# The even mixer of a two-block network as one stream on TensorE, its output product in two passes

## The reference

```python
def mixer_even(x, w_in, gla_wg2, gla_bg, gla_norm_g, w_o):
    gq, gk, gv, gg, gr, dq, dk, dv = _split(x @ w_in, EVEN_SPLITS)   # 512 512 1024 16 1024 1536 1536 1536
    o_a = gla(gq, gk, gv, gg, gla_wg2, gla_bg)          # 4 heads, keys 128, values 256
    o_a = rms_norm(o_a, gla_norm_g) * jax.nn.silu(gr)
    for g, (window, dilation) in enumerate(DIL_PAIRS):  # 3 groups x 4 heads x 128
        o_g, lse_g = dilated_branch(dq[:, :, g], dk[:, :, g], dv[:, :, g], window, dilation)
    wts = jax.nn.softmax(jnp.stack(lses, 0), axis=0)
    o_b = jnp.sum(wts[..., None] * jnp.stack(outs, 0), axis=0)
    return jnp.concatenate([o_a, o_b], axis=-1) @ w_o

def gla(q, k, v, g1, w_g2, b_g):                        # chunks of 64 tokens
    log_a = jax.nn.log_sigmoid(g1 @ w_g2 + b_g) / GLA_TAU
    b = jnp.cumsum(log_a, axis=2)
    q_dec, k_inv, k_end = q * dk ** -0.5 * exp(b), k * exp(-b), k * exp(b_last - b)
    o_intra = tril(q_dec @ k_inv.T) @ v
    s_loc = k_end.T @ v                                 # states, then a scan with the decay
    return o_intra + q_dec @ s_prev
```

## Time and profile before

| | us |
|---|---|
| three runs | 3624.05, 3625.61, 3627.94 (median 3625.61) |
| the profiled execution | 3624.08 |
| its span, first to last instruction | 3622.2 |
| TensorE busy in the span | 3477.5 (96%) |
| VectorE, ScalarE busy | 1951.2 (54%), 1618.7 (45%) |
| stretch between the input and the output projection of the even mixer | 352.72 to 459.89 |

### The profile page before, as it was taken

One profiled execution on the slowest core, in us unless ns is written; L12 is line 12 of the kernel. 1 busy time (PEld: TensorE's weight loads), 2 busy tenths in 40 slices (PEclk: granted clock), 3 DMA queues, 4 the chain that ended last, 5 costly groups with the idle time before them and its releaser, 6 DMA issues.

```text
span 3622.2 us, 43342 instructions
## 1 busy us (share of the span) xinstructions
PE 3477.5 (96%) x15818; PEld 2837.3 (78%) x15818; DVE 1951.2 (54%) x2307; ACT 1618.7 (45%) x2052; POOL 288.8 (8%) x402
## 2 busy tenths in 40 slices
PE   8999689999999989999999999999989899999997
PEld 7887578888888778777888878877878778888886
DVE  4444365555555565666575544557544745555555
ACT  4444234444444346553444444436545544444443
POOL 0000000000000000001291003000270000000000
PEclk9999799999999999999999999999999999999998
DMA  7665056665655555446655656655544456566663
GB/s 244 188 189 163 1 174 205 198 190 180 198 187 182 175 156 176 123 153 174 197 183 182 197 162 204 201 173 177 182 152 125 147 176 190 190 189 191 190 190 105
DMA packets 335046, 630.04 MB, mean 174 GB/s; under 512 B 33212, under 2 KB 35488, under 8 KB 333392
## 3 DMA queue, kind: packets, MB, share of 16 engines
q1 hardware_dynamic: 330416, 611.59, 54.4%
q0 software_dynamic: 4512, 16.86, 1.5%
HBM read 624.99 MB, written 2.33 MB: 173 GB/s over the span
## 4 chain that ended last, share of the span: by engine, by line
PE 90%; DVE 4%; POOL 3%; ACT 1%; issue 1%; DMA 0%; SPq 0%; DVEq 0%; ACTq 0%
PE psum L259 27%; PE psum L261 27%; PE psum L260 27%; PE psum L329 2%; POOL big L1274 1%; PE psum L510 1%; PE psum L512 1%; PE psum L511 1%; DVE weights_lo L221 1%; POOL scratch L1276 1%; POOL scratch L1275 1%; PE psum L918 0%; DVE x L1889 0%; PE psum L2754 0%; DVE x L1938 0%
## 5 line engine op out<-in xcount | busy, mean ns | idle before, releaser
L221 DVE TENSOR_TENSOR weights_lo<-weights_raw,weights_hi 128x1024 fp32r<-128x1024 f32 x1155 | 1419.4, 1244 | 1174.9 <-ACT weights_hi L214 1173.7
L214 ACT CAST weights_hi<-weights_raw 128x1024 fp32r<-128x1024 f32 x1155 | 1208.3, 1050 | 1653.3 <-PE psum L261 1633.0
L259 PE MATMUL psum<-weights_hi,act_hi 128*128 128x512 f32 x3112 | 1234.2, 397 | 12.8 <-DVE weights_lo L221 8.4
L261 PE MATMUL psum<-weights_hi,act_lo 128*128 128x512 f32 x3112 | 1216.4, 391 | 0.0
L260 PE MATMUL psum<-weights_lo,act_hi 128*128 128x512 f32 x3112 | 1215.2, 390 | 0.0
L259 PEld LDWEIGHTS psum<-weights_hi,act_hi 128*128 128x128 f32 x3112 | 586.7, 189 | 135.5 <-issue 15.2
L261 PEld LDWEIGHTS psum<-weights_hi,act_lo 128*128 128x128 f32 x3112 | 586.1, 188 | 124.7
L260 PEld LDWEIGHTS psum<-weights_lo,act_hi 128*128 128x128 f32 x3112 | 586.9, 189 | 116.9
L259 PE MATMUL psum<-weights_hi,hid_hi 128*128 128x512 f32 x1336 | 532.6, 399 | 16.6 <-DVE weights_lo L221 15.3
L260 PE MATMUL psum<-weights_lo,hid_hi 128*128 128x512 f32 x1336 | 523.2, 392 | 0.0
L261 PE MATMUL psum<-weights_hi,hid_lo 128*128 128x512 f32 x1336 | 523.1, 392 | 0.0
(11 more groups left out here) (396 smaller groups left out, 1796.2 us busy)
## 6 DMA issues: line engine op xcount, KB each, us to landing
weights_raw<-in_ffn_wgu SPq DMA_DIRECT2D x352, 512.0 KB, 4.4
weights_raw<-in_w_ff SPq DMA_DIRECT2D x256, 512.0 KB, 4.2
weights_raw<-in_ffn_wd SPq DMA_DIRECT2D x176, 512.0 KB, 3.8
weights_raw<-in_even_w_in SPq DMA_DIRECT2D x120, 512.0 KB, 3.7
weights_raw<-in_odd_w_in SPq DMA_DIRECT2D x64, 512.0 KB, 3.7
weights_raw<-in_w_in SPq DMA_DIRECT2D x64, 512.0 KB, 3.8
weights_raw<-in_odd_w_o SPq DMA_DIRECT2D x32, 512.0 KB, 3.8
weights_raw<-in_w_out SPq DMA_DIRECT2D x32, 512.0 KB, 3.8
```

Source lines behind the costliest of these rows:

```text
L214: nc.scalar.copy(w_hi[:, u % SPLIT_SLOTS, :size], raw[:, u % RAW_SLOTS, :size]).then_inc(hi_ready, 1)
L221: nc.vector.tensor_tensor(w_lo[:, u % SPLIT_SLOTS, :size], raw[:, u % RAW_SLOTS, :size], w_hi[:, u % SPLIT_SLOTS, :size].bitcast(F32), ALU ...
L259: nc.tensor.matmul(o, ah, wh, start=(k + j == 0), stop=False)
L261: last = nc.tensor.matmul(o, al, wh, start=False, stop=(k + j == kts - 1))
```

## The change

Everything of the even mixer now stands as side work in one stream of 137 units (`mixer_stage`, `EVEN_ENDS`). The tile `proj_e` is gone: each block goes to where it is used, q, k and the dilated q, k by way of one block-wide tile `raw_e` and turns two and three units later. Columns are loaded in the order q, k, gate, v, v, r, r, dilated q, k, v. The gate's steps have units 18 to 30, the states 36 to 42, the eight items 44 to 53, the dilated turns 58 to 99, the wide items' scores 101 to 115 and turns 103 to 118. The output product becomes a first pass over the eight gated tiles (units 121 to 136, from `hid_hi`), with the wide items' products beside it at units 123 to 130, and a second pass over the four dilated tiles (units 137 to 144). Each pass adds into x. The minimum of the negated scores replaces the maximum and its negation. The constants are loaded after the lead's turns; the vectors of the first layer norm when the first wide item is done.

```diff
@@ SyncE
+        for col, cols in ((G_K, BLK), (G_G, 16), (G_V, BLK), (G_V + BLK, BLK)):
             block_load(sp, c, w, 0, KT_D, col, cols)
...
-        project(A["even_w_o"][0], 0, [(BLK * j, BLK) for j in range(1, 4)], 12)
+        for j in range(11):
+            block_load(sp, c, w, 0, KT_D, G_R + j * BLK, BLK)
+        for row, kts in ((0, 8), (1024, 4)):
+            for j in range(4):
+                block_load(sp, c, A["even_w_o"][0], row, kts, j * BLK, BLK)
@@ GpSimd
+        pool.wait_ge(turned, LEAD)
...
-        pool.wait_ge(att_done, 8)
+        pool.wait_ge(att_done, 1)
         vectors(0, "ln1", 0)
@@ the stage
+    EVEN_ENDS = [8, 16, 17, 25, 33, 41, 49, 57, 65, 73, 81, 89, 97, 105, 113, 121, 125, 129, 133, 137]
+    EVEN_BLOCKS = [(KT_D, BLK), (KT_D, 16)] + [(KT_D, BLK)] * 13 + [(8, BLK)] * 4
@@ ScalarE, even_act: e is the unit that TensorE has just done
+            if e in (7, 15, 56, 64, 72, 80, 88, 96):
+                evac_at(act, c, e, b, lambda m, o: nc.scalar.copy(raw_e[:, m, :], o))
...
+            if e in (104, 112, 120):
+                g = (e - 104) // 8
+                evac_at(act, c, e, b, lambda m, o: nc.scalar.copy(dv[:, m, g, :], o))
+            i = (e - 102) // 2
+            if 0 <= i < 8 and e % 2 == 0:
+                least, total, _ = (d_stat[:, k, i:i + 1] for k in range(3))
+                act.wait_ge(att_scaled, i + 1)
+                of = d_sc[:, i % 2, 0:384 * (i % 2 + 1)]
+                A_(of, of, ACT.Exp, bias=least, scale=-1.0, accum_out=total).then_inc(att_exped, 1)
+            if wide_turn(e) is not None:
+                i, (t0, _) = wide_turn(e)
+                act_turn(act, c, wide_pt(i, t0, 3))
@@ VectorE
+        mixer_stage(c, even_dve, EVEN_ENDS)
+        mixer_splits(unit_lo, dve, c, EVEN_BLOCKS)
+        residual(4, 1, None)
+        c.stage(None)
...
@@ VectorE, even_dve
+            if e in (124, 128, 132, 136):
+                q = slice((e - 124) // 4 * BLK, (e - 120) // 4 * BLK)
+                evac_at(dve, c, e, b, lambda m, o: STT(out=x[:, m, q], in0=x[:, m, q], scalar=ALPHA, in1=o,
+                                                       op0=ALU.mult, op1=ALU.add))
@@ TensorE, even_pe: v is the unit just done
+            if v in (9, 10, 17, 18, 58, 59, 66, 67, 74, 75, 82, 83, 90, 91, 98, 99):
+                at_v = max(a for a in (9, 17, 58, 66, 74, 82, 90, 98) if a <= v)
+                if v == at_v:
+                    taken(pe, c, v - 2)
+                tiles(raw_e, 2 * (v - at_v))
...
+            if wide_turn(v) is not None:
+                i, (t0, t1) = wide_turn(v)
+                if t0 == 0:
+                    pe.wait_ge(att_exped, i + 1)
+                c.item_turn[i] = c.n["turn"]
+                turn(pe, c, [d_sc[:, i % 2, t * P:(t + 1) * P] for t in range(t0, t1)])
+            i = (v - 101) // 2
+            if 0 <= i < 8 and v % 2:
+                h, m = i // 2, i % 2
+                if i == 0:
+                    all_turned()
+                else:
+                    pe.wait_ge(att_scaled, i)
+                nk = P * (m + 1)
+                flat = psum[:, 6:8, :].rearrange("p b n -> p (b n)")
+                for g in range(3):
+                    last = MM(flat[:, g * nk:(g + 1) * nk], dqT[:, 4 * g + h, m * P:(m + 1) * P], dkT[:, 4 * g + h, :nk],
+                              start=True, stop=True)
+                last.then_inc(att_scored, 1)
+            i = v - 123
+            if 0 <= i < 8:
...
+                for t in range(3 * (m + 1)):
+                    last = MM(psum[:, 6 + i % 2, 0:P], wide_pt(i, t), dv[:, t % (m + 1), t // (m + 1), h * P:(h + 1) * P],
+                              start=(t == 0), stop=(t == 3 * m + 2))
+                last.then_inc(att_pved, 1)
...
+        for _ in range(4):
+            block_mm(pe, c, 8, BLK, hT_hi, hT_lo)
+        all_turned()
+        c.stage(None)
+        for _ in range(4):
+            block_mm(pe, c, 4, BLK, aT_hi, aT_lo)
```

761 lines of the change are left out of this document (292 added, 469 removed).

## The result

The changed kernel takes **3573.28 us** (median of four runs, 3571.5 to 3576.83), the kernel before 3625.05: a ratio of 0.9857, 95% interval 0.984 to 0.9874. The forecast was 3582, the range 3566 to 3600. The profiled execution took 3576.83 us with a span of 3574.6; this was the longest of its four runs; the first experiment shows where most of that lies.

A forecast was written before the change was run, and what follows sets the result against it. A chain of short steps over three engines bounds the gap, TensorE the stream. Costs 56.6 + 1.5 + 8.1 + 2.5 = 68.7, less 109.7 and 2.5, give -43.5 us: 3582 us, range 3566 to 3600.

The forecast's parts named there:

- turns of four tiles, 24: Even mixer's stream: 24 four-tile turns moved between units cost 0.48 us each, 11.5 us.
- four local states: Even mixer's stream: four states of three half-height products cost 1.26 us each, 5.0 us.
- gated items: Even mixer's stream: eight masked score and output items cost 11.5 us, plus 3.0 for entering at ten places, 14.5.
- wide items with the waits on exponentials: Even mixer's stream: 72 blocks at 0.30 us and 36 turned tiles cost 25.6 us; exponentials add 1.5 of waiting.
- second pass, waits: Output product: TensorE waits 5.3 us after the first short block and 1.4 at two others, 8.1 in all.
- second pass, clock and the rest: Output product: slow products at a reduced clock behind the 5.3 us wait cost 2.5 us, between 0 and 2.8.
- start: Kernel start: loading masks and constants after the lead's turns brings x sooner, saving 2.5 us, between 0 and 3.5.
- What bounds it: Old even mixer: a chain of short steps over three engines bounds the gap, TensorE the stream; 109.7 us open to change.
- forecast's upper bound of 62 us: Attention work in the stream: 0.4 us more at all 30 entries with products beyond the bare passes, against 56.6 expected.
- Free steps: Even mixer: norm gain, gate product and first-pass adds hide on ScalarE or VectorE inside units; uncovered adds would be 5.1 us.
- stream did not leak: Rival, wide items: ScalarE one unit later at each of eight returns 22 us, 3604 us (3592 to 3612); chance 0.15.
- Cheaper than counted: Rival, whole change: no entry cost, clock stays, long wait only 1.4, best start; 3567 us (3560 to 3568); chance 0.12.

The follow-up runs named there:

- the first experiment: The changed kernel run once more, unaltered, as yardstick for the variants beside it; 3573.16 us, ratio 0.9859 to the kernel before.
- evac_first: The changed kernel with VectorE evacuating the first pass's last output block one unit earlier, ahead of the second pass's first add; 3568.22 us, ratio 0.9846.
- late_add: evac_first, plus each second-pass add of the even mixer placed behind both splits of its two-unit block; 3565.97 us, ratio 0.9836.
- warm_tail: The changed kernel plus twenty identity products on TensorE between the second pass's first two blocks, inside the 5.02 us wait; 3571.13 us, one execution.

## Why the prediction was right, point by point

The change of the profiled executions was -47.3 us (3624.08 to 3576.83), and of the medians -51.8; forecast -43.5. Of the 8.3 us between -43.5 and -51.8, 5.3 lie up to the last output product (-48.8), the rest of the program took 1.2 back, and the other 4 are the distance of the two profiled executions from their medians, which is luck. The mechanism and the places were right; the sizes:

| term | predicted us | measured us |
|---|---|---|
| turns of four tiles, 24 | 11.5 | 11.5 (24 x 0.48) |
| four local states | 5.0 | 5.1 |
| gated items | 14.5 | 11.6 |
| wide items with the waits on exponentials | 25.6 + 1.5 | 22.8 |
| second pass, waits | 8.1 | 7.2 |
| second pass, clock and the rest | 2.5 | 2.9 |
| start | -2.5 | -0.7 |

A turn is measured as in the earlier trace rows: a unit with one in front recurs after 3.20 us (215.06 to 218.27, 250.60 to 253.81). The measured rows above the start sum to 61.1 us; from the lead turn at 30.98 to 478.90 are 447.9 us, less 321.1 + 65.3 at the bare pace 61.5. So 0.4 us are not assigned. The parts, point by point:

- **What bounds it.** Right. The gap was handing round, not work: put among the units the same work costs about 51 us where the gap and its surplus took 109.7. From the first input product to the last output product it is 465.6 us (13.23 to 478.86), forecast 472.
- **Gated items.** From the first score at 153.33 to the unit at 185.52 lie eight units (21.8 us) and seven of the eight products' items, so 10.4; with the last, 11.6. The row of 1.43 us per item held; of the 3.0 us added for entries 0.2 are left.
- **Wide items.** From the unit at 322.35 to the one at 429.95 are 107.6 us with 31 units (84.3); less one turn of the output 22.8, waits included. What was mis-sized is the price of a block, 0.30 us from the odd mixer's items: they hold two products over 64 rows, which cost 0.28 and 0.29 us more for the changes of height. Without these (3.04 - 0.57 - 0.33)/9 is 0.24, and in the even mixer, whose wide items have none, it is 0.24 too (22.8 less 1.5 of waits and 4.0 for 36 tiles, over 72), of which 0.22 is the block. The earlier trace rows had shown 0.24; it was taken as the lower bound and was the nearer row, since it is of operations that moved. These two terms, gated and wide items, are the 7 us by which the stream beat the forecast. The forecast's upper bound of 62 us can't be redone: 0.4 us at 30 entries on top of 48.5 is 60.5.
- **Waits on exponentials.** 1.5 in sum, as predicted, but 0.78 for the one with the table load in front (predicted 0.4) and 0.37 twice (predicted 0.5).

The row of ScalarE behind the first of them, in the changed kernel:

```profile
332.95 1.28 ACT L1392 ACT_TABLE_LOAD   x1
334.24 0.61 ACT L1392 ACTIVATE big<-big,big 128x384 f32<-128x384 f32 x1
```

The exponential starts 1.29 us after the load began. The Trainium skill (ScalarE: Activation LUTs, "What ACT_TABLE_LOAD costs") has 2.66 us with a drain; by that the wait would have been 2.2 us. The trace disagrees again.
- **Second pass.** One wait of 5.02 (predicted 5.3) and two of 1.10 (predicted 1.4), in the order predicted, shown by evac_first and late_add. The clock behind the long one 1.9 (predicted 2.5), shown by warm_tail. The remaining 1.0 of the tail is in slower first products and in the pace's rounding; I didn't take it apart.
- **Free steps.** Right: TensorE has no wait in the stream but those for the exponentials, so the gain, the gate and the adds of the first three blocks are covered. The add of the fourth is the one that the long wait was for.
- **Start.** The step that failed. Its rows gave 1.1 us and 2.5 were taken, with no row for the rest. The turn of x's second quarter came 1.4 us earlier (12.49 against 13.87), but ten of the twelve products behind it ran at half clock, where in the kernel before it was six: the net gain was 0.7 us. That the clock would eat half of the gain was not in the prediction. With fillers the turn behind them comes 1.2 to 2.5 us earlier.
- **The rest of the program** was taken as unchanged. The profiled pair has +1.2 us there, with 3.2 us of half clock in the odd mixer that the kernel before didn't have. Against it, TensorE's clock came back sooner behind the same waits: from the product behind the 3.02 us in the first feed-forward layer to the next one that waited it was 12.32 us before (1257.44 to 1269.76), 11.15 after, with the same instructions.
- **Rivals.** The stream did not leak. "Cheaper than counted" had its first part nearly right (entries 0.1 us and less), its other three (clock stays, long wait only 1.4, start 1 us better) not.

## What to carry to other kernels

Work of a latency-bound gap costs little between units of a full engine: price it by rows of the same operations, with the same shapes, at full clock, and add at most 0.1 us for entering. Then look at what a shorter block does to the engine that serves it: when a block is only two units deep, an add and its statistics between two splits are 1.1 us of waiting a time, and behind both splits none. Where TensorE waits anyway for some microseconds, look whether products behind the wait run at half clock: here filler products gave back 1.9 us in one place and 1.2 to 2.5 in another, each in one execution.

## What the runs showed of the hardware

- Twenty products of a 128-column identity keep TensorE's clock at full level through a wait of 5 us (behind them 0.40 us per product, without them 0.63), and bring it there at the start (0.47 and 0.39 from the first product on).
- Without them the clock's return falls at different times in executions of the same instructions: the turn behind the first twelve products came between 17.01 and 18.32 us in nine profiles that differ only later. A wait of 1.83 us in the odd mixer was followed by five to eight products at half clock in ten of thirteen profiles and by none in three; in the one measured that cost 1.6 us.
- A row of 22 records of one-column products at 1482.90 was followed by the half clock in one execution and in no other, 1.6 us.
- A 64-row product between 128-row ones cost 0.28 to 0.29 us more than one of 128 rows, with 256 columns and with 128: the weight loads at both changes of height were not hidden under the product before.
